# Value products of the expert layer: the order of the halves of gathered rows, and the count that frees their slots

## The chip, the cores and the metric

The kernel runs on one core of one Trainium2 chip, everything in 32-bit floats. The metric is the device time of one launch in microseconds, as the median of repeated runs. The engines are named as the profile names them: PE is the tensor engine's matmul, PEld its weight load, DVE the vector engine, ACT the scalar engine, POOL the GpSimd engine, SP the queue that issues the loads of weights.

## The reference, cut to what matters

The reference is a two-layer decoder trunk for 256 prompt tokens and 8 sample tokens of width 1024. In each layer a mixer (matrix-memory LSTM heads and causal pooling) is followed by an expert layer and by a gated per-layer embedding. The change touches the expert layer alone, which picks 16 single-neuron experts in each of 8 heads of every token out of tables of 16384 rows:

```python
def block_fn(xb):                                   # 128 tokens
    ...
    eidx = jnp.take_along_axis(cidx, sel, axis=-1)  # token, head, 16
    gate = jax.nn.softmax(top, axis=-1)
    ue = u_tab[eidx]
    act = jax.nn.gelu(jnp.einsum('td,thkd->thk', xb, ue).astype(jnp.float32))
    ve = v_tab[eidx]
    return jnp.einsum('thk,thkd->td', (gate * act).astype(xb.dtype), ve)
```

So every token needs 128 rows of `u` (a dot product each) and 128 rows of `v` (their weighted sum). The rows of 1024 floats come from HBM by index.

## The kernel before

**Tiles and passes.** The tokens of a layer are three tiles: A (tokens 0 to 127), B (128 to 255) and S (the 8 samples). Over the two layers they are tiles 0 to 5. The expert layer runs in four passes: tile 0; tiles 1 and 2; tile 3; tiles 4 and 5. In each pass all gathers of `u` come first, then all of `v`.

**Gathers.** POOL issues 1056 gathers in the fixed order `GATHERS` (the loop from line 1427, the DMA at 1450). One gather brings 128 rows of 1024 floats, one for each partition, 512 KB, into slot n % 14 of the ring `rows` (`RING` = 14). Below, "a row" is the content of one such slot. For `u`, row i holds expert i of each of the tile's 128 tokens. For `v`, the index is transposed: one row holds the 128 experts of one token. Gather n raises `row_in[n % 14]` by 16 when it has landed. Before POOL issues gather n it waits until the slot's last content, gather n - 14, has been used: by the count `u_used`, which DVE raises with each row (line 2105), or by the count `v_used`, which PE raises. `V_BY` (lines 617 to 620) counts for every gather how many `v` rows there are up to it; before the change POOL turns that into groups of four (line 1447).

**Dots.** DVE multiplies a `u` row by the normalised tokens and sums it (line 2105), one instruction for each row.

**Value products.** `vals(t, g)` (lines 1196 to 1237) handles `GROUP` = 4 rows, thus four tokens. PE waits until all four have landed (lines 1212 and 1213). Row i's product is a matmul with 32 columns of weights in `wz`, of which one is not zero, so that the sum lands in one partition of `acc`; the four rows of a group write to the four blocks of 32 partitions. `acc` has 1024 columns in two PSUM banks of 512, so each row takes two matmuls, its first half (c = 0) and its second half (c = 1). All four first halves come first, then all four second halves, and the last matmul raises `v_used` by one for the group:

```python
for c in range(2):
    for i in range(GROUP):
        ...
ins.then_inc(v_used, 1)
```

Each such fp32 matmul shows in the trace as two MATMUL and two weight-load records, 16 MATMULs to a group. There are 122 groups of this kind (32 for each of tiles 0, 1 and 3, and 26 for tile 4). The last 6 groups of tile 4 ("late") and the two groups of each S tile go another way (lines 1214 to 1229): each row is four matmuls of 256 columns, one for each block of 32 partitions, and again one raise of `v_used` for a group. These are 10 groups.

**Who waits for `v_used`.** POOL before it reuses a slot (line 1447); DVE's `refill` (line 2140) after group 16 of a tile, when it puts the second half of the weights into `wz`; DVE's `gelu` of an S tile and its `weights`, which wait for an earlier tile's last group; and `add_experts` (line 2144), which adds `acc` to the residual once `all_added(t)` (lines 632 and 633) is reached.

**What sets the order.** Every engine runs a list of steps (`SCHEDULE`) that a planner has woven from step costs when the kernel is built: "vals" is taken as 1.8 us of PE, "dots" as 1.31 us of DVE for each row, and a slot is taken as free at the end of its group (lines 477 to 480). While tile 0's and tile 3's `v` rows are summed, PE and DVE also work through the next tiles' mixer, queries and expert choice, with weights that SP loads into a ring of three 1 MB slots. In the last part of tile 1's and tile 4's `v` rows PE has nothing else to do.

Of the kernel before, what the change touches and what calls it, by code (L numbers as in the profile page):

```python
# [30 lines left out]
BLOCK = 512  # L31
# [11 lines left out]
RING = 14  # L43
GROUP = 4
DOTS = 2
QUAD = 32
TURN = QUAD // 2
# [65 lines left out]
def layer_of(tile):  # L113
    return tile // 3
# [147 lines left out]
def own_groups(t):  # L262
    late = LATE if t == PASS_TILES[-1][0] else 0
    return ROWS_V[KIND[t]] // GROUP - late
# [34 lines left out]
PLACE = {g: n for n, g in enumerate(GATHERS)}  # L299
# [281 lines left out]
def count(stages, entry):  # L581

    n = 0
    for e in SCHEDULE:
        n += e[0] in stages
        if e == entry:
            return n
    raise KeyError(entry)


def chosen_by(tile, head):

    n = 0
    for e in SCHEDULE:
        n += e[0] == ("choose" if KIND[tile_of(e)] == "S" else "best") if e[0] in ("best", "choose") else 0
        if e[:2] == ("choose" if KIND[tile] == "S" else "best", tile) and e[2] <= head < e[3]:
            return n
    raise KeyError(tile)
# [18 lines left out]
U_BY, V_BY = [], []  # L617
# [5 lines left out]
def token(tile, i):  # L623

    return i if KIND[tile] == "S" else QUAD * (i % 4) + i // 4
# [4 lines left out]


def all_added(tile):
    return V_BY[PLACE["v", tile, own_groups(tile) * GROUP - 1]] // GROUP


def lane_of(tile, i):

    if KIND[tile] == "S":
        return i
    return DEC + LATE * (i % GROUP) + i // GROUP - own_groups(tile)  # L640
# [28 lines left out]
def build(nc, a):  # L669
    with ExitStack() as ctx:  # L670
        def sb(name, *shape, dt=F32):
            return ctx.enter_context(nc.sbuf_tensor(name, list(shape), dt))

        def sem(name):
            return ctx.enter_context(nc.semaphore(name))
# [3 lines left out]
        rows = sb("rows", P, RING, D)  # L679
# [24 lines left out]
        v = {"A": sb("v", P, HEADS, HD + 1), "S": sb("v_s", P, HD + 1)}  # L704
# [69 lines left out]
        wz = sb("wz", P, 4, TURN * (QUAD + 1) + TURN)  # L774
# [3 lines left out]
        acc = ctx.enter_context(nc.psum_tensor("acc", [P, 2, BLOCK], F32))  # L778
# [14 lines left out]
        half_used, u_used, v_used = sem("half_used"), sem("u_used"), sem("v_used")  # L793
# [27 lines left out]
        def lane_group(g):  # L821
            return slice(g * LANE, (g + 1) * LANE)
# [9 lines left out]
        def window(g, lane):  # L832

            return (QUAD + 1) * (g % TURN) + TURN - lane
# [8 lines left out]
        def emptied(eng, *name):  # L843

            b, n = use[name]
            eng.wait_ge(bank_free[b], n + 1)  # L846

        @block.tensor
        def _(pe):
# [346 lines left out]
            def vals(t, g):  # L1196

                kind = KIND[t]
                if g == 0:
                    if kind != "S":  # L1200
                        emptied(pe, "turn_w", t)
                    else:
                        pe.wait_ge(weight_done, t + 1)
                    if t > 0:
                        pe.wait_ge(acc_read, t)
                if kind != "S" and g == TURN:
                    pe.wait_ge(refilled, count(("refill",), ("refill", t)))
                late = g >= own_groups(t)
                if late:
                    pe.wait_ge(acc_read, t + 1)  # L1210
                n = PLACE["v", t, g * GROUP]
                for i in range(GROUP):
                    pe.wait_ge(row_in[(n + i) % RING], 16 * ((n + i) // RING + 1))
                if kind == "S" or late:
                    lanes_from = own_groups(PASS_TILES[-1][0]) if layer_of(t) == DEPTH - 1 else 0
                    first = g == (lanes_from if late else 0) and (late or not lanes_from)
                    for i in range(GROUP):
                        row = rows[:, (n + i) % RING, :].rearrange("p (c s n) -> p c s n", c=2, s=4)
                        lane = lane_of(t, g * GROUP + i)
                        if late:  # L1220
                            at = window(g, lane)
                            weights_of = wz[:, i, at:at + LANE]
                        else:
                            weights_of = wz_s[:, lane * LANE:(lane + 1) * LANE]
                        for s in range(4):
                            ins = pe.matmul(acc[lane_group(s), 0, 0:HALF], weights_of, row[:, :, s, :],
                                            start=first and i == 0, stop=kind == "S" and lane == DEC - 1, skip_group_check=True)
                    ins.then_inc(v_used, 1)
                    return
                first, end = g == 0, g + 1 == own_groups(t)  # L1230
                for c in range(2):
                    for i in range(GROUP):
                        row = rows[:, (n + i) % RING, c * BLOCK:(c + 1) * BLOCK]
                        at = window(g, g)
                        ins = pe.matmul(acc[i * QUAD:(i + 1) * QUAD, c, :], wz[:, i, at:at + QUAD], row,  # L1235
                                        start=first, stop=end, skip_group_check=True)
                ins.then_inc(v_used, 1)

            def turn3(t):
                pe.wait_ge(acc_read, t + 1)  # L1240
# [185 lines left out]
        @block.gpsimd  # L1426
        def _(pool):
            pool.memset(wz[:, :, :], 0.0).then_inc(wz_clear, 1)
            pool.memset(wz_s[:, :], 0.0).then_inc(wz_clear, 1)
            for n, (table, t, i) in enumerate(GATHERS):  # L1430
                kind = KIND[t]
                if kind == "S" and table == "u" and i == 0:
                    emptied(pool, "turn_s", t)
                if kind != "S" and table == "u" and i % TOPK == 0:

                    pool.wait_ge(index_ready, chosen_by(t, i // TOPK))
                if kind != "S" and table == "v" and i == 0:
                    emptied(pool, "turn_index", t)
                if n >= RING:

                    old = GATHERS[n - RING]
                    if old[0] == "u" and KIND[old[1]] == "S":
                        emptied(pool, "copies", old[1], old[2], 1)
                    elif old[0] == "u":
                        pool.wait_ge(u_used, U_BY[n - RING])
                    else:
                        pool.wait_ge(v_used, (V_BY[n - RING] + GROUP - 1) // GROUP)
                at = i if table == "u" else token(t, i)
                which = index[kind] if table == "u" else index_t[kind]
                pool.indirect_dma_start(  # L1450
                    out=rows[:, n % RING, :], out_offset=None, in_=a[table],
                    in_offset=bass.IndirectOffsetOnAxis(ap=which[:, at:at + 1], axis=0),
                ).then_inc(row_in[n % RING], 16)
# [233 lines left out]
        def _(dve):  # L1687
# [422 lines left out]
            def gelu(t):  # L2110

                kind = KIND[t]
                dve.wait_ge(gelu_done, t + 1)
                if t == 0:
                    dve.wait_ge(wz_clear, 2)
                if kind == "S":
                    if t > 2:
                        dve.wait_ge(v_used, all_added(t - 3))
                    by_token = wz_s[:, :].rearrange("p (b c) -> p b c", c=LANE + 1)[:, :, 0:1].rearrange("p b o -> p (b o)")
                    after(dve.tensor_tensor(by_token, dots["S"][:, :], prob["S"][:, :], ALU.mult), weight_done)  # L2120
                    return
                after(dve.tensor_tensor(dots[kind][:, :], dots[kind][:, :], prob[kind][:, :], ALU.mult), weight_done)

            def by_token():
                placed = wz[:, :, TURN:].rearrange("p j (r c) -> p j r c", c=QUAD + 1)[:, :, :, 0:1]
                return placed.rearrange("p j r o -> p j (r o)")
# [10 lines left out]

            def refill(t):

                dve.wait_ge(v_used, V_BY[PLACE["v", t, TURN * GROUP - 1]] // GROUP)  # L2140
                after(dve.tensor_copy(by_token(), w_later[:, :, :]), refilled)  # L2141

            def add_experts(t):
# [181 lines left out]
```

## Time and profile before

| what | value |
|---|---|
| median of 3 runs | 1913.62 us (1909.67 to 1915.09) |
| span of the profiled execution | 1891.7 us |
| PE busy | 1079.0 us, 57% of the span |
| DVE busy | 978.1 us, 52% |
| POOL busy | 998.2 us, 53% |
| DMA queue of the gathers | 75.9% of the 16 DMA engines' span |
| HBM traffic | 362 GB/s over the span |
| mean granted TensorE clock | 0.752 of full |

The page gives the span of the profiled execution, from its first to its last instruction, and no time of its own beside it. The median lies 21.9 us above that span, which is what lies around the instructions, and the scatter from run to run. No engine is busy for 60% of the span, while the DMA engines' share is at 9 tenths or just under in most of the page's 40 slices. The stretches with `v` rows are, in us of the span: tile 0's rows from 340 to about 570; tile 1's from about 810 to 996; tile 3's from 1250 to 1472; tile 4's from 1696 to 1870, the last of them late groups and the S rows of tile 5.

### The profile page before, as it was taken

How to read it: one execution, taken by the hardware profiler on the slowest of the kernel's cores; microseconds unless marked ns; L12 is line 12 of the kernel's file. 1: busy time of each engine (PE TensorE's matmuls, PEld its weight loads, DVE VectorE, ACT ScalarE, POOL GpSimd, SP SyncE). 2: the span in 40 equal slices, each digit the busy share in tenths (PEclk: the TensorE clock that was granted, in tenths of full speed). 3: DMA queues.
4: the chain of work that ended last, by engine and by line, in shares of the span. 5: the costliest groups of instructions: out<-in, count | busy, mean ns of one | idle time of the engine just before them, and what ended most of it. 6: DMA issues, size and time to landing. Idle time of an engine off the chain costs nothing. (4 is left out here: it accounts for less than half of the span.)

```text
span 1891.7 us, 17959 instructions
## 1 busy us (share of the span) xinstructions
PE 1079.0 (57%) x6318; PEld 499.7 (26%) x6318; DVE 978.1 (52%) x2585; ACT 192.3 (10%) x332; POOL 998.2 (53%) x1062
## 2 busy tenths in 40 slices
PE   8840257788955835385655874048885522045556
PEld 4420133433412422241112432024341211031113
DVE  1498975523445788954004576951344497850001
ACT  3200021201101200000000212000110000000002
POOL 0156534345465555656666353755446566656663
PEclk9965668789987967697676886578896765576678
DMA  8699869889999999989999799979999999999995
GB/s 333 244 359 379 337 244 410 337 359 399 357 360 406 423 410 421 404 343 419 371 366 386 256 421 365 408 286 418 368 337 366 402 374 381 396 330 372 368 367 206
DMA packets 172759, 685.11 MB, mean 362 GB/s; under 512 B 19616, under 2 KB 21344, under 8 KB 158190
## 3 DMA queue, kind: packets, MB, share of 16 engines
q0 software_dynamic: 152064, 553.72, 75.9%
q1 hardware_dynamic: 20606, 130.25, 17.3%
q8 instruction: 51, 0.84, 0.2%
q14 instruction: 38, 0.31, 0.0%
HBM read 677.66 MB, written 6.59 MB: 362 GB/s over the span
## 5 line engine op out<-in xcount | busy, mean ns | idle before, releaser
L2105 DVE SCALAR_TENSOR_TENSOR rows<-rows,acc 128x1024 f32<-128x1024 f32 x512 | 594.2, 1217 | 49.6 <-issue 26.7
L908 PE MATMUL bank<-wring,turned 128*128 128x512 f32 (+1 forms) x808 | 394.0, 635 | 40.6 <-DMA wring<-in_w 24.3
L1235 PE MATMUL acc<-rows,wz 128*32 128x512 f32 x1952 | 323.1, 783 | 143.6 <-DMA rows<-in_v,index_tb 102.6
L1450 POOL DMA_INDIRECT rows<-in_u,index_A x256 | 240.3, 939 | 303.2 <-DVE rows L2105 123.8
L1450 POOL DMA_INDIRECT rows<-in_v,index_ta x256 | 242.5, 947 | 234.1 <-PE acc L1235 142.2
L1450 POOL DMA_INDIRECT rows<-in_u,index_B x256 | 240.7, 940 | 179.1 <-DVE rows L2105 110.7
L1450 POOL DMA_INDIRECT rows<-in_v,index_tb x256 | 241.1, 942 | 138.7 <-issue 68.1
L908 PEld LDWEIGHTS bank<-wring,turned 128*128 128x128 f32 x808 | 160.5, 207 | 236.7 <-issue 205.7
L1235 PEld LDWEIGHTS acc<-rows,wz 128*32 128x32 f32 x1952 | 69.6, 130 | 351.9 <-issue 347.0
L1185 PE MATMUL bank<-xn_s,consts 128*128 128x128 f32 x256 | 48.6, 334 | 154.3 <-issue 154.3
L1185 PEld LDWEIGHTS bank<-xn_s,consts 128*128 128x128 f32 x256 | 42.9, 243 | 159.9 <-issue 159.9
L2151 DVE TENSOR_TENSOR x_b<-x_b,acc 128x1024 f32<-128x1024 f32 x2 | 2.4, 1222 | 155.8 <-issue 89.9
L905 PE MATMUL bank<-wring,turned_s 128*32 128x128 f32 x1568 | 64.9, 281 | 27.1 <-issue 27.0
L1959 DVE MAX8 top<-scratch 128x8 f32<-128x128 f32 x66 | 15.0, 282 | 120.9 <-ACT scratch L1604 119.6
L905 PEld LDWEIGHTS bank<-wring,turned_s 128*32 128x32 f32 x1568 | 44.8, 111 | 69.7 <-issue 69.6
L2141 DVE COPY wz<-w_later 128x64 f32<-128x64 f32 x4 | 0.9, 225 | 101.4 <-PE acc L1235 77.7
L1109 PE MATMUL bank<-consts,qk 128*128 128x128 f32 x64 | 12.5, 324 | 68.7 <-issue 66.3
L1194 PE MATMUL bank<-consts,dots_A 128*128 128x128 f32 x2 | 1.0, 476 | 76.6 <-issue 74.6
L2105 DVE DVE_READ_ACCUMULATOR rows<-rows,acc 128x1 f32 x512 | 42.0, 82 | 3.6 <-issue 3.6
L1136 PE MATMUL bank<-consts,top 128*128 128x128 f32 (+2 forms) x10 | 3.9, 393 | 61.9 <-DVE top_f L1993 61.9
L1259 PE MATMUL bank<-wring,emb 128*128 128x512 f32 x32 | 19.9, 781 | 26.8 <-issue 13.6
L2169 DVE TENSOR_TENSOR xn<-xn,bank 128x512 f32<-128x512 f32 x6 | 4.1, 689 | 59.9 <-PE bank L1259 59.9
(320 smaller groups left out, 1054.4 us busy)
## 6 DMA issues: line engine op xcount, KB each, us to landing
wring<-in_w SPq DMA_DIRECT2D x103, 1024.0 KB
out_sample<-scratch SPq DMA_DIRECT2D x2, 2128.5 KB
scratch<-in_c_s SPq DMA_DIRECT2D x2, 2064.0 KB
rows<-in_u,index_A POOLq DMA_INDIRECT x256
rows<-in_v,index_ta POOLq DMA_INDIRECT x256
rows<-in_u,index_B POOLq DMA_INDIRECT x256
rows<-in_v,index_tb POOLq DMA_INDIRECT x256
kept<-in_w SPq DMA_DIRECT2D x2, 1024.0 KB
```

The source lines that it names most:

```text
L905: ins = pe.matmul(ps[lane_group(g), 0:P], turned["S"][:, 4 * h + c, :], w[:, c, g * P:(g + 1) * P], start=first, stop=end, skip_group_chec ...
L908: ins = pe.matmul(ps[:, part], turned["A"][:, 4 * h + c, :], w[:, c, part], start=first, stop=end, skip_group_check=True)
L1109: ins = pe.transpose(ps[:, i * P:(i + 1) * P], pq[:, 0, i * P:(i + 1) * P], const("ident"))
L1136: ins = pe.transpose(ps[0:m, i * P:(i + 1) * P], src[:, 2 * h0:2 * h1, :].rearrange("p l k -> p (l k)"), const("ident"))
L1185: ins = pe.matmul(ps[:, g * P:(g + 1) * P], const("ident")[:, lane:lane + 1].to_broadcast([P, P]), xn["S"][:, i * P:(i + 1) * P], start=Tr ...
L1235: ins = pe.matmul(acc[i * QUAD:(i + 1) * QUAD, c, :], wz[:, i, at:at + QUAD], row, start=first, stop=end, skip_group_check=True)
L1259: ins = pe.matmul(ps[:, :], emb[:, c, 0:P], w[:, 2 * j + c, :], start=(c == 0), stop=(c == 1))
L1450: pool.indirect_dma_start(out=rows[:, n % RING, :], out_offset=None, in_=a[table], in_offset=bass.IndirectOffsetOnAxis(ap=which[:, at:at + ...
L1959: highest = [marked(dve.max(values[:, 0:half], src)) for values, _, src in lists]
L2105: dve.scalar_tensor_tensor(u, u, 1.0, acc[:, :, :], ALU.mult, ALU.mult, accum_out=dots[kind][:, s:s + 1]).then_inc(u_used, 1)
L2151: after(dve.tensor_tensor(sum_, sum_, acc[:, :, :], ALU.add), acc_read)
L2169: free(dve.tensor_tensor(sig, sig, ps[:, 0:n], ALU.mult), "embed", t, j)
```

## The change

Three things change, and no other instruction, load or step is added, removed or moved:

1. `v_used` counts rows instead of groups. `all_added` and the waits of POOL and of `refill` are rewritten for that.
2. In the 122 ordinary groups PE waits for each row just ahead of its first half. The eight matmuls come in the order (row, half): (0,0) (1,0) (0,1) (2,0) (1,1) (3,0) (2,1) (3,1), and each second half raises `v_used`.
3. In the late groups and the groups of the S tiles PE waits for each row ahead of its four matmuls, and `v_used` is raised after each row.

```diff
 def all_added(tile):
-    return V_BY[PLACE["v", tile, own_groups(tile) * GROUP - 1]] // GROUP
+    return V_BY[PLACE["v", tile, own_groups(tile) * GROUP - 1]]
...
-                for i in range(GROUP):
+
+                def landed(i):
                     pe.wait_ge(row_in[(n + i) % RING], 16 * ((n + i) // RING + 1))
+
                 if kind == "S" or late:
...
                         lane = lane_of(t, g * GROUP + i)
+                        landed(i)
                         if late:
...
-                    ins.then_inc(v_used, 1)
+                        ins.then_inc(v_used, 1)
                     return
                 first, end = g == 0, g + 1 == own_groups(t)
-                for c in range(2):
-                    for i in range(GROUP):
-                        row = rows[:, (n + i) % RING, c * BLOCK:(c + 1) * BLOCK]
-                        at = window(g, g)
-                        ins = pe.matmul(acc[i * QUAD:(i + 1) * QUAD, c, :], wz[:, i, at:at + QUAD], row,
-                                        start=first, stop=end, skip_group_check=True)
-                ins.then_inc(v_used, 1)
+                at = window(g, g)
+
+                def half_product(i, c):
+                    row = rows[:, (n + i) % RING, c * BLOCK:(c + 1) * BLOCK]
+                    return pe.matmul(acc[i * QUAD:(i + 1) * QUAD, c, :], wz[:, i, at:at + QUAD], row,
+                                     start=first, stop=end, skip_group_check=True)
+
+                for i in range(GROUP):
+                    landed(i)
+                    half_product(i, 0)
+                    if i:
+                        half_product(i - 1, 1).then_inc(v_used, 1)
+                half_product(GROUP - 1, 1).then_inc(v_used, 1)
...
-                        pool.wait_ge(v_used, (V_BY[n - RING] + GROUP - 1) // GROUP)
+                        pool.wait_ge(v_used, V_BY[n - RING])
...
-                dve.wait_ge(v_used, V_BY[PLACE["v", t, TURN * GROUP - 1]] // GROUP)
+                dve.wait_ge(v_used, V_BY[PLACE["v", t, TURN * GROUP - 1]])
```

## Rows read from the trace of the kernel before

**Rows 1.** The page: busy time by engine, and the gathers' queue.

```profile
PE 1079.0 (57%) x6318; PEld 499.7 (26%) x6318; DVE 978.1 (52%) x2585; ACT 192.3 (10%) x332; POOL 998.2 (53%) x1062
...
q0 software_dynamic: 152064, 553.72, 75.9%
```

**Rows 2.** The page, costliest groups: line, engine, tiles, busy us, mean ns, idle before.

```profile
L1235 PE MATMUL acc<-rows,wz 128*32 128x512 f32 x1952 | 323.1, 783 | 143.6 <-DMA rows<-in_v,index_tb 102.6
```

**Rows 3.** The waits of the whole span: us in total, times, longest us.

```profile
POOL rows L1450 <- PE acc L1235: 171.0, 49, 13.3
```

**Rows 4.** Windows: length, PE, PEld, DVE, ACT, POOL busy (instructions), clock, DMA share, GB/s.

```profile
340.00:520.00 180.00, 149.00 (x1109) 71.48 (x1113) 69.27 (x282) 24.58 (x48) 83.27 (x88) 0.91 0.93 360
...
880.00:996.00 116.00, 63.52 (x344) 13.07 (x339) 1.45 (x2) 0.00 (x0) 76.41 (x82) 0.72 0.98 375
...
1600.00:1656.00 56.00, 0.66 (x2) 0.23 (x1) 46.40 (x79) 0.00 (x0) 36.60 (x40) 0.50 1.01 400
```

**Rows 5.** Windows of line 1235 alone: PE and PEld busy, clock, DMA share, GB/s.

```profile
340.00:520.00 180.00, 52.04 (x360) 11.70 (x364) 0.91 0.93 360
520.00:570.00 50.00, 24.50 (x156) 5.42 (x148) 0.79 0.97 358
...
880.00:996.00 116.00, 63.48 (x340) 12.99 (x332) 0.72 0.98 375
1250.00:1420.00 170.00, 51.83 (x368) 12.04 (x368) 0.89 0.92 352
1420.00:1472.00 52.00, 27.48 (x148) 5.48 (x144) 0.67 0.98 372
1696.00:1827.00 131.00, 70.57 (x368) 14.48 (x368) 0.70 0.97 369
```

**Rows 6.** The waits between 340 and 520 us.

```profile
POOL rows L1450 <- PE acc L1235: 73.8, 15, 13.3
```

**Rows 7.** The waits between 880 and 996 us.

```profile
PE acc L1235 <- DMA rows<-in_v,index_tb: 43.7, 17, 5.0
...
POOL rows L1450 <- remote: 13.4, 5, 3.3
...
POOL rows L1450 <- PE acc L1235: 4.4, 3, 2.6
```

**Rows 8.** The timeline of POOL in the stretch of tile 4.

```profile
1739.03 0.93 POOL L1450 DMA_INDIRECT rows<-in_v,index_tb  x1 [0.31 <-issue]
1743.36 0.94 POOL L1450 DMA_INDIRECT rows<-in_v,index_tb  x1 [3.39 <-PE acc L1235]
...
1766.20 0.93 POOL L1450 DMA_INDIRECT rows<-in_v,index_tb  x1 [3.29 <-PE acc L1235]
```

**Rows 9.** The timeline of POOL in the u stretch before it.

```profile
1645.92 0.94 POOL L1450 DMA_INDIRECT rows<-in_u,index_B  x1 [0.46 <-DVE rows L2105]
```

**Rows 10.** The timeline of PE: start, duration, count of instructions, idle before.

```profile
380.17 5.36 PE L1235 MATMUL acc<-rows,wz 128*32 128x512 f32 x48
...
1734.56 3.64 PE L1235 MATMUL acc<-rows,wz 128*32 128x512 f32 x16 [2.45 <-issue]
1739.47 3.64 PE L1235 MATMUL acc<-rows,wz 128*32 128x512 f32 x16 [1.26 <-issue]
```

**Rows 11.** The timeline of PE at the end.

```profile
1824.51 1.92 PE L1235 MATMUL acc<-rows,wz 128*32 128x512 f32 x16 [2.58 <-DMA rows<-in_v,index_tb]
...
1869.40 3.64 PE L1226 MATMUL acc<-rows,wz_s 128*32 128x256 f32 x32 [4.86 <-DMA rows<-in_v,index_S]
1876.75 3.39 PE L1226 MATMUL acc<-rows,wz_s 128*32 128x256 f32 x32 [3.71 <-DMA rows<-in_v,index_S]
```

**Rows 12.** The timeline of POOL at the end.

```profile
1849.71 1.40 POOL L1450 DMA_INDIRECT rows<-in_v,index_tb  x1 [4.26 <-PE acc L1226]
```

**Rows 13.** The timeline of DVE at the end.

```profile
1834.47 1.22 DVE L2151 TENSOR_TENSOR x_b<-x_b,acc 128x1024 f32<-128x1024 f32 x1 [65.89 <-remote]
...
1880.25 0.42 DVE L2146 TENSOR_TENSOR x_s<-x_s,acc 128x256 f32<-128x256 f32 x1 [14.89 <-PE acc L1226]
```

## The prediction

> **What bounds the kernel now.** I first read the page's busy times [rows 1]. No engine is near its span, while the queue of the gathers takes 75.9% of the DMA engines' time. Line 1235, the value products, has PE idle 143.6 us ahead of it, 102.6 of them until tile B's rows land [rows 2], while POOL waits 171.0 us in 49 pieces for those products to free slots [rows 3]. So each waits for the other, in different places. The average hides two kinds of stretch, so I read it by windows next [rows 4], then for line 1235 alone [rows 5].
>
> In the **woven** stretches, 340 to 520 and 1250 to 1420 us, PE is busy 149.00 of 180 us with the next tiles' work and the value products are a third of that (52.04). No wait of line 1235 on a DMA shows among the waits there; instead POOL waits 73.8 us for the products to free slots [rows 6]. The rows are there before PE is, and PE's own list of steps sets the pace. In the **landing-paced** stretches, 520 to 570, 880 to 996, 1420 to 1472 and 1696 to 1827, PE has only the products, is busy 63.52 of 116 us, and waits 17 times, 43.7 us in sum, for a row to land [rows 4, 7]. The DMA share is 0.97 to 0.98. By MATMUL records these stretches hold (156 + 340 + 148 + 368) / 4 = 253 rows [rows 5], four records to a row. All of tile 1's and tile 4's ends lie on the path that sets the end.
>
> The pace there is 82 gathers in 116 us, 1.415 us a row [rows 4]; between two marks of POOL 16 gathers apart, 1743.36 and 1766.20, it is 22.84 / 16 = 1.43 [rows 8]. POOL could issue every 0.93 + 0.31 = 1.24 us, and once in 16 gathers it stands still for 3.3 us, released by PE or by a source the trace calls remote [rows 7, 8]. The question is whether that stop costs anything. The gather stream without PE answers it in part: in the u stretch from 1600 to 1656 slots are freed row by row, and 40 gathers take 56 us, 1.40 us each, with a short wait at each one [rows 4, 9]. So freeing by the row changes the shape of the waiting, from one long stop to many short ones, and the rate hardly.
>
> **Part one, slots freed by the row, landing-paced stretches.** A group's passes now begin with the landing of its fourth row, and all slots come free 3.64 us later at the low clock [rows 10]. After the change the first row is used while the others still land. Its slot comes free about 4 us sooner, the second and third less, the fourth not at all. POOL has 14 slots in flight; a group that is waiting or being used holds at most four rows and 3.64 us of landing, under three more, so at least seven transfers are still queued. DMA engines that have seven transfers waiting don't stand still. The gain then is 1.42 less 1.40 for 253 rows: 0.02 x 253 = 5 us. The bounds are 0 (the pace is the engines' own) and 253 x (1.42 - 1.24) = 45 us (POOL's own pace). I take 5, since the u row is the nearest to it: the same size of gather, the same ring, and one signal for each row. By the late signals it would be more: the group whose slot POOL wants at 1743.36 had ended before 1739.47, so the stop is partly a signal that arrives late. Row-by-row signals may be just as late.
>
> **Part two, the order of the halves.** The work is the same: eight matmuls, 16 records. At the low clock a group takes 3.64 us for 16 records of 1.06 us each at most, so the four blocks of 32 partitions run side by side, in four rounds of 0.9 us; at the high clock three groups in a row take 5.36 us, 1.79 each, 0.45 a round [rows 10]. The skewed order still has four records for each block, so four rounds are the least. In the landing-paced stretches the first three rows' rounds move into time in which PE idles now. The fourth row needs its four rounds after it has landed as before, so a group's end doesn't move, unless the clock does. The granted clock is 0.72 there [rows 4], a mean over times at 1.2 and at 2.4 GHz, with PE stopping for 1.3 to 2.8 us between groups. With rows used as they land the stops are shorter and more; the clock could be granted for longer. The gain is at the ends of tiles: at most 3.64 - 1.92 = 1.7 us at each of four [rows 10, 11], nothing where the last group is fast already, as tile 4's is (1.92 at 1824.51). I take 1.5 us for all.
>
> In the woven stretches all four rows are there, so nothing starts sooner and all four blocks finish in the same round: I put the order and the earlier signals at nothing. POOL's 73.8 us of waiting there [rows 6] is for PE's other work, and rows that come in sooner only lie longer. That is covered by PE's list; if products ran one after another instead, the first slot would come free up to three quarters of 1.79 us sooner and POOL's waits would shrink, still without moving PE.
>
> **Part three, late and S groups.** POOL waits for whole groups of line 1226, 4.26 us at 1849.71 [rows 12], and what comes last is the landing of the S rows: PE waits 4.86 and 3.71 us for them [rows 11], and DVE's last addition follows at 1880.25 [rows 13]. Freed by the row, the first slot of a group opens about three quarters of its length sooner, 1.4 us by the 1.92 us of a fast group [rows 11]. PE also uses S rows 0 to 2 of a group while the fourth lands, but the end needs the fourth. I take 1.5 us, between 0 and 4.
>
> **Part four, the waits and the signals.** 396 raises of a count are added, three in each of 132 groups. PE's four waits are the same four. A wait now stands between matmuls; what is queued behind it in the group's list is the second half of a row that has landed, (1,1) behind the third row and so on, and in the woven stretches nothing waits. A raise is priced by no row. Its bounds: 0, and the 0.13 us by which a single fast group (1.92) exceeds one of a packed three (1.79) [rows 10, 11]. I take 0: in the landing-paced stretches it lies in idle time, and a raise by another block's matmul need not hold the rest.
>
> The Trainium skill speaks against this part: "TensorE: Matmul & The Clock Gate", section "The cost: per-tile semaphore tail", has each raise take 26.3 ns one after another and advises one on the last matmul. By that rule 396 raises would be 10.4 us, an estimate, and the sum would be 1916. No row of this trace has several raises in one group, so it neither confirms nor refutes it.
>
> **The sum.** -5 - 1.5 - 1.5 = -8 us. The profiled execution goes from 1891.7 to 1883.7; the median of runs lies 21.9 above its span, and 1913.6 - 8 = 1905.6, say 1906. From no change, a measurement of this kernel tells about 0.3%, 5.7 us.
>
> **The rivals.** *Stops that cost their length.* If the 3.3 us stops do bind, the gathers speed up to what the engines can carry. From 1600 to 1656 they moved 400 GB/s, against 375 [rows 4]; 0.524 MB at 400 GB/s is 1.31 us, 0.11 less than now, 28 us over 253 rows, and with the 3 us of the other parts the time is 1883. For it: the stop has the length of two and a half gathers, and the DMA engines have carried more than they do here. Against it: the share is 0.98 already, the extra in that stretch was loads of weights, and the gathers were at 1.40. 0.15.
>
> *Slower: the order costs PE rounds.* The four blocks run side by side only if PE reaches past matmuls that wait for their block. Now the fourth block's first record stands behind three that can't start yet; in the skewed order (3,0) stands behind seven (the second records of (0,0), (1,0), (2,0), both of (0,1) and of (1,1)). If PE doesn't reach so far, the fourth block starts two rounds late and a group takes six rounds. That is 2 x 0.45 = 0.9 us for each of (360 + 368) / 16 = 45 woven groups, 41 us, in stretches where PE is busy for 83% and its list sets the pace [rows 4, 5]; with half of it hidden in PE's pauses, +20, so 1926. In the landing-paced stretches it is hidden. It decides from about 0.3 us a group upwards, where it passes the gain. For it: the order of issue is all that makes the blocks overlap. Against it: PE does overlap four blocks across three packed groups. 0.18.
>
> The Trainium skill, page "TensorE: Matmul & The Clock Gate", section "The mechanism" of the part on packing small matmuls, has matmuls start and end strictly in the order of issue. In this order two records of one block follow each other, so a strict order would need nine rounds for a group, 4.0 us by 0.45, and the packed three took 1.79 each [rows 10]: the trace disagrees, and so this rule doesn't count against the new order either.
>
> *The raises cost.* Half of the upper bound, 0.065 x 3 in 45 woven groups, 9 us: 1915. 0.10, half of it beyond what counts as no change.
>
> *Nothing.* The engines carry what they can (share 0.98), the ends don't move, 1913. POOL's waits change shape only. 0.17.
>
> **How the numbers follow.** My forecast, 1906, has 0.40, a fifth of it within 5.7 us of no change. Faster: 0.32 + 0.15 = 0.47. Within: 0.08 + 0.17 + 0.05 = 0.30. Slower: 0.18 + 0.05 = 0.23. The range reaches to the first rival below, 1880, and to the second above, 1925; left out are more than that gain and the slow order at more than half its price. The likeliest case alone spans 1899 to 1911.
>
> **What would show it.** In the profile after: the stops at every 16th gather gone and POOL's waits short and many; gathers from 880 to 996 and from 1696 to 1827 at 1.40 us a row (my forecast), 1.31 or less (the first rival) or 1.42 (nothing); woven groups at 1.79 us in a row of three, or 2.7 (the slow order); the clock in the landing-paced stretches; DVE's addition of tile 4 at about 6 us before 1834.47. I am wrong if the woven stretches change in length by more than 3 us, or the GB/s of the landing-paced ones passes 385.

## The result and the profile after

The changed kernel takes 1933.82 us (median of 4 runs, 1929.70 to 1940.54) beside 1911.64 us for the kernel before in the same comparison. The ratio is 1.0092, with a 95% interval of 1.0047 to 1.0138: slower by about 1%, where I had forecast 1906 us and 0.4% faster. Two more comparisons on other occasions gave 1.0105 (1.0056 to 1.0155) and 1.0108 (1.0061 to 1.0155). One profiled execution scatters by about as much as the effect: the changed kernel's three profiles span 1938.7, 1903.1 and 1919.7 us. So single rows of one profile show here how something happens, and only ratios say what it costs. The profiled execution of 1938.7 us took 1940.54 us by its own time, 1.8 us more than its span; the 21.9 us that the forecast added to the span of the profile before were therefore mostly scatter between executions.

The page after, as in [rows 1, 2], with the value products now at line 1238:

```profile
PE 1155.1 (60%) x6318; PEld 519.0 (27%) x6318; DVE 978.1 (50%) x2585; ACT 192.3 (10%) x332; POOL 997.8 (51%) x1062
...
q0 software_dynamic: 152064, 553.72, 75.1%
...
L1238 PE MATMUL acc<-rows,wz 128*32 128x512 f32 x1952 | 394.3, 671 | 61.8 <-issue 31.8
```

PE is busy 76 us longer, nearly all of it in the products (323.1 to 394.3 us). Their idle time fell more than that, from 143.6 to 61.8 us, and nothing was won. Over the whole span POOL waits a little longer for the products than in [rows 3], in 77 pieces instead of 49:

```profile
POOL rows L1459 <- PE acc L1238: 194.5, 77, 11.5
```

The windows of the same stages: tile 0's woven stretch, and the landing-paced ones of tiles 1 and 4 (columns as in [rows 4]):

```profile
355.00:535.00 180.00, 143.94 (x1052) 66.36 (x1053) 61.71 (x240) 19.45 (x38) 77.60 (x82) 0.87 0.88 327
907.00:1023.00 116.00, 92.49 (x332) 17.59 (x324) 0.23 (x1) 0.00 (x0) 76.56 (x82) 0.97 0.98 374
1742.00:1873.00 131.00, 102.93 (x365) 20.36 (x362) 0.22 (x1) 0.00 (x0) 85.87 (x92) 0.96 0.97 366
```

In the landing-paced stretch of tile 1 there are again 82 gathers in 116 us, at 374 GB/s (375 before) and a share of 0.98: the same number of gathers in the same time as in [rows 4]. PE is busy 92.49 us there instead of 63.52 and its clock is granted at 0.97 instead of 0.72. For line 1238 alone (to be held against [rows 5]):

```profile
355.00:535.00 180.00, 52.01 (x336) 12.76 (x336) 0.87 0.88 327
907.00:1023.00 116.00, 92.49 (x332) 17.59 (x324) 0.97 0.98 374
```

The timelines show how. In the landing-paced stretch PE now starts with each row, so it hardly stops and stays at the high clock:

```profile
939.49 1.05 PE L1238 MATMUL acc<-rows,wz 128*32 128x512 f32 x4 [0.18 <-DMA rows<-in_v,index_tb]
940.71 1.05 PE L1238 MATMUL acc<-rows,wz 128*32 128x512 f32 x4 [0.17 <-DMA rows<-in_v,index_tb]
941.97 2.28 PE L1238 MATMUL acc<-rows,wz 128*32 128x512 f32 x8 [0.20 <-issue]
```

POOL's one stop of 3.3 us in 16 gathers [rows 8] has become several of 1.4 to 2.1 us, the rate is unchanged:

```profile
946.74 0.94 POOL L1459 DMA_INDIRECT rows<-in_v,index_tb  x1 [1.54 <-PE acc L1238]
949.56 0.94 POOL L1459 DMA_INDIRECT rows<-in_v,index_tb  x1 [1.88 <-remote]
...
958.14 0.93 POOL L1459 DMA_INDIRECT rows<-in_v,index_tb  x1 [1.40 <-remote]
...
967.42 0.94 POOL L1459 DMA_INDIRECT rows<-in_v,index_tb  x1 [2.13 <-remote]
```

In the woven stretch three groups in a row take 5.38 us, against 5.36 in [rows 10]. The skewed order costs PE nothing; but 18 us later PE waits 8.55 us for ACT:

```profile
390.90 5.38 PE L1238 MATMUL acc<-rows,wz 128*32 128x512 f32 x48
...
408.50 1.92 PE L1089 MATMUL bank<-pooled_s,w_pool 128*128 128x32 f32 x8 [8.55 <-issue]
```

That wait is where I first saw something of the loss. Here are the two pieces of ACT's work that release these matmuls (the pooling of tile B and of the samples), in the kernel before:

```profile
358.57 0.60 ACT L1569 ACTIVATE decayed<-bank 128x512 f32<-128x512 f32 x1 [5.72 <-PE bank L1078]
...
390.94 0.28 ACT L1569 ACTIVATE pooled_s<-bank 128x128 f32<-128x128 f32 x1 [3.77 <-PE bank L1067]
```

and after:

```profile
370.69 0.60 ACT L1578 ACTIVATE decayed<-bank 128x512 f32<-128x512 f32 x1 [11.18 <-remote]
...
408.17 0.28 ACT L1578 ACTIVATE pooled_s<-bank 128x128 f32<-128x128 f32 x1 [10.27 <-remote]
```

PE's last matmul of the first group of inputs (line 1078) and the matmul that waits for ACT:

```profile
364.14 0.29 PE L1078 MATMUL bank<-consts,u_a 128*128 128x16 f32 x2
371.35 2.08 PE L1089 MATMUL bank<-decayed,w_pool 128*128 128x128 f32 x8 [6.91 <-ACT decayed L1578]
```

PE's input for ACT's step was done at 364.14 + 0.29 = 364.43 us, and ACT began at 370.69, 6.3 us later. The profile finds no instruction that ended just before, and calls the releaser "remote". PE then stood 6.91 us. The trace's semaphore events settle what ACT waited for: the count that PE's matmul raises changed at 370.61 us. The completion of a matmul was reported six microseconds after its end. The second time the matmul ended at 399.95 and its raise was seen at 408.09, 8.1 us late. POOL was in an unbroken run of 12 gathers, which ends at 407.68, and ACT started at 408.17:

```profile
393.07 0.94 POOL L1459 DMA_INDIRECT rows<-in_v,index_ta  x1 [10.16 <-PE acc L1238]
394.31 0.93 POOL L1459 DMA_INDIRECT rows<-in_v,index_ta  x1 [0.30 <-issue]
...
406.74 0.94 POOL L1459 DMA_INDIRECT rows<-in_v,index_ta  x1 [0.30 <-issue]
```

The same at the end of tile 0: the last product ends at 587.40 + 1.90 = 589.30, DVE's addition starts at 597.79.

```profile
587.40 1.90 PE L1238 MATMUL acc<-rows,wz 128*32 128x512 f32 x6 [1.05 <-DMA rows<-in_v,index_ta]
599.07 1.33 PE L884 MATMUL bank<-consts,x_a 128*128 128x128 f32 x5 [9.76 <-DVE x_a L2160]
```

```profile
597.79 1.22 DVE L2160 TENSOR_TENSOR x_a<-x_a,acc 128x1024 f32<-128x1024 f32 x1 [20.78 <-remote]
```

```profile
594.00 0.94 POOL L1459 DMA_INDIRECT rows<-in_u,index_B  x1 [0.30 <-issue]
597.79 0.93 POOL L1459 DMA_INDIRECT rows<-in_u,index_B  x1 [2.86 <-remote]
```

The semaphore events show the raises of `v_used` too. Here are those at that place, with the ends of the matmuls that make them and POOL's gathers (worked out from the trace, in us):

```
matmul ends    584.57 584.57 584.60 584.61   586.28 586.35 588.45 589.30
raise seen     586.21 587.66 589.80 591.91   597.53 597.59 597.65 597.70
gathers begin  585.31 586.55 587.80 589.04 590.28 591.52 592.76 594.00, stop, 597.79
```

While POOL issues, the raises come out singly, 1.4 to 2.1 us apart, up to 7.3 us late. After POOL has stopped, four come within 0.17 us, the oldest of them 11.3 us late. Over tiles 0 and 1 of the kernel before, a raise whose matmul ended during a run of gathers was seen 2.4 us late on average, one outside a run 0.4; after the change it was 4.2 and 0.9. (Raises and ends were paired in order; about 7% of the raises are missing from the trace, so these are estimates.) This rise lies in tile 1: by another pairing, the one with the least sum of delays, an estimate too, raises in a run were 2.8 us late in tile 1 before the change and 5.1 after, but 1.9 and 2.7 in tile 0. The experiments find no loss in tile 1 (e6 below), so the rise from 2.4 to 4.2 is not a measure of the loss.

### The profile page after: what moved, and what is told of

It is laid out like the page before. It is cut to its first block and busy times, and to the rows that moved or that the text cites. A ratio compares the mean times of both kernels' runs of the same rounds, so it can differ in the third digit from the quotient of the medians.

```text
span 1938.7 us, 17710 instructions
## 1 busy us (share of the span) xinstructions
PE 1155.1 (60%) x6318; PEld 519.0 (27%) x6318; DVE 978.1 (50%) x2585; ACT 192.3 (10%) x332; POOL 997.8 (51%) x1062
## 5 line engine op out<-in xcount | busy, mean ns | idle before, releaser
L1238 PE MATMUL acc<-rows,wz 128*32 128x512 f32 x1952 | 394.3, 671 | 61.8 <-issue 31.8
L1238 PEld LDWEIGHTS acc<-rows,wz 128*32 128x32 f32 x1952 | 87.0, 117 | 325.5 <-issue 204.1
L905 PE MATMUL bank<-wring,turned_s 128*32 128x128 f32 x1568 | 76.6, 290 | 45.8 <-issue 45.7
L905 PEld LDWEIGHTS bank<-wring,turned_s 128*32 128x32 f32 x1568 | 48.8, 115 | 93.0 <-issue 92.7
L1136 PE MATMUL bank<-consts,top 128*128 128x128 f32 (+2 forms) x10 | 3.9, 393 | 63.5 <-DVE top_f L2002 62.1
L1658 ACT ACTIVATE turned<-bank 128x512 f32<-128x512 f32 x8 | 4.8, 597 | 303.8 <-issue 161.3
L1120 PE MATMUL bank<-keys,q_t 128*128 128x128 f32 x128 | 22.5, 327 | 14.1 <-issue 10.8
```

The lines of the kernel that those rows point to most:

```text
L905: ins = pe.matmul(ps[lane_group(g), 0:P], turned["S"][:, 4 * h + c, :], w[:, c, g * P:(g + 1) * P], start=first, stop=end, skip_group_chec ...
L1120: ins = pe.matmul(ps[:, i * P:(i + 1) * P], pqT[:, i, :], keys[:, 4 * block_of(j) + i, :], start=True, stop=True)
L1136: ins = pe.transpose(ps[0:m, i * P:(i + 1) * P], src[:, 2 * h0:2 * h1, :].rearrange("p l k -> p (l k)"), const("ident"))
L1238: return pe.matmul(acc[i * QUAD:(i + 1) * QUAD, c, :], wz[:, i, at:at + QUAD], row, start=first, stop=end, skip_group_check=True)
L1658: free(act.activation(turned[KIND[t]][:, i * c:(i + 1) * c, :], ps[:, 0:c * m].rearrange("p (h c) -> p h c", h=c), ACT.Copy), "turn3", t, i)
```

## The experiments

All ratios are to the kernel before, from runs of the same comparison, with 95% intervals. "By the row" means one raise of `v_used` for each row, "by the group" one for four.

**The parts of the change alone.** e1 takes the changed kernel's raises and slots with the old order:

```diff
                 for i in range(GROUP):
                     landed(i)
-                    half_product(i, 0)
-                    if i:
-                        half_product(i - 1, 1).then_inc(v_used, 1)
-                half_product(GROUP - 1, 1).then_inc(v_used, 1)
+                for i in range(GROUP):
+                    half_product(i, 0)
+                for i in range(GROUP):
+                    half_product(i, 1).then_inc(v_used, 1)
```

> The old order and the old wait for four rows, but each second half raises the count and slots are freed by the row (396 more raises, slots as in the changed kernel). Theory 1, the raises: PE's completions already reach POOL and DVE several us late at the ends of tiles, and more raises make them later, for everybody who waits on PE; the ratio to before is that of the change, 1.008 to 1.014, about 1930 us. Theory 2, the order with its waits between matmuls: no loss, 0.997 to 1.002. Theory 3, slots freed earlier send gathers into the loads of weights: as theory 1 here, 1.008 to 1.014.

Measured: 1.0116 (1.0067 to 1.0164). The whole loss, without the new order.

e2 is the mirror: the new order and its waits, one raise for each group, `V_BY[...] // GROUP` in the waits as before.

```diff
-                        half_product(i - 1, 1).then_inc(v_used, 1)
+                        half_product(i - 1, 1)
```

> The new order with its waits row by row, but one raise for each group as before. Theory 1 (raises): no loss, 0.995 to 1.001. Theory 2 (order and waits): the whole loss, 1.008 to 1.014. Theory 3 (slots freed earlier): no loss.

Measured: 0.9994 (0.9961 to 1.0028). The order costs nothing and brings nothing. Theory 2 is out.

e3 is e1, but POOL waits for all four raises of a group:

```diff
-                        pool.wait_ge(v_used, V_BY[n - RING])
+                        pool.wait_ge(v_used, (V_BY[n - RING] + GROUP - 1) // GROUP * GROUP)
```

> The old order and waits, four raises for each group, but POOL waits for all four, so slots come free as before and only the number of raises differs. Theory 1 (raises): the whole loss, 1.008 to 1.014. Theory 2 (order): none, 0.998 to 1.002. Theory 3 (slots freed earlier): none.

Measured: 1.0033 (0.9991 to 1.0074). Theory 1 as I had put it falls too: the same raises as in e1 cost between nothing and 0.7% when POOL still waits for whole groups, not the whole loss; the value lies between the ranges of the theories. Freeing slots by the row makes up the rest, 0.8% by the middle values.

e4 is the changed kernel once more:

> The changed kernel once more, beside before on one chip. All theories: 1.005 to 1.014, and a second profile of it. Theory 1 expects again that DVE's additions at the ends of tiles 0 and 3 start 6 us or more after the last product, where before they followed within 0.2 us; if they don't, these late signals are chance.

Measured: 1.0105 (1.0056 to 1.0155). In its profile DVE's addition comes 4.9 us after the last product of tile 0 and 8.8 after that of tile 3: late again, though less than the 6 us that I had expected for tile 0.

**Where it costs.** e5 and e6 count by the row in some tiles only, with the new order everywhere. In e5:

```diff
+def BY_ROW(t, i):
+    return t in (0, 3)
...
-    V_BY.append((V_BY or [0])[-1] + (_g[0] == "v"))
+    V_BY.append((V_BY or [0])[-1] + (_g[0] == "v" and (BY_ROW(_g[1], _g[2]) or _g[2] % GROUP == 0)))
```

and the raises in `vals` to match; in e6 `t not in (0, 3)`.

> The changed kernel, but a raise and a free slot for each row only in tiles 0 and 3, whose products are woven with other work; tiles 1, 4 and the S tiles raise once a group. The new order stays everywhere. Theory A (PE's completions leave in order and slowly while POOL issues gathers, so extra raises delay the completions that ACT, DVE and POOL wait for; this costs where other engines wait on PE, in the woven stretches): nearly the whole loss, 1.007 to 1.013. Theory B (each extra raise costs the same wherever it stands): half of it, 1.004 to 1.006. Theory C (the loss comes from the landing-paced stretches and tile 4's end): 0.998 to 1.002.

> The mirror image: by the row in tiles 1, 4 and the S tiles, once a group in tiles 0 and 3. Theory A: 0.996 to 1.003. Theory B: 1.004 to 1.006. Theory C: 1.007 to 1.013. If it is below 0.997, freeing by the row pays where only the gathers set the pace.

Measured: e5 1.0108 (1.0060 to 1.0156), e6 1.0009 (0.9982 to 1.0036). The whole loss is in tiles 0 and 3, where other engines wait for PE while POOL gathers. In tiles 1 and 4, where the gathers set the pace, freeing by the row costs and gains nothing that can be told, at most 0.2%; most of my forecast's 5 us lay there.

e7 raises the count with all eight matmuls of a group, in the old order, POOL waiting for whole groups:

```diff
-                    half_product(i, 0)
+                    half_product(i, 0).then_inc(v_used, 1)
```

> The old order and waits, all eight matmuls of a group raise the count, and POOL waits for the whole group: 122 x 4 = 488 raises more than with four for a group (which gave 1.0033). Theory A and B, the raises themselves: 1.006 to 1.015. Theory D (what costs is that slots come free early, by the row, and the raises nothing): 1.000 to 1.004, as with four raises.

Measured: 1.0051 (1.0019 to 1.0082). It lies between the ranges of the theories, so it decides neither way.

e8 is the kernel before, again:

> The kernel before once more: 0.998 to 1.002 by every theory. Its second profile tells whether completions of PE at the ends of tiles 0 and 3 come late in it too (in the first profile DVE's additions followed the last product within 0.2 us; with the new order and one raise, 6 us or more late).

Measured: 0.9957 (0.9924 to 0.9989), which misses what an unchanged kernel should give: a difference of 0.4% can be chance in these comparisons. So e3 and e7 suggest that the raises themselves cost something, but don't show it. Its profile also takes away a reading of mine: late completions are in the kernel before as well. PE's two waits for ACT at the place of the first trace, in e8:

```profile
370.48 2.08 PE L1089 MATMUL bank<-decayed,w_pool 128*128 128x128 f32 x8 [6.30 <-ACT decayed L1569]
...
402.25 1.92 PE L1089 MATMUL bank<-pooled_s,w_pool 128*128 128x32 f32 x8 [2.54 <-ACT pooled_s L1569]
```

6.30 and 2.54 us, against 6.91 and 8.55 after the change; in the first profile of before they were 1.73 and 1.84. The two waits sum to 7.6 to 15.5 us with slots by the row in tile 0 (after, e1, e4, e5, e16) and to 3.6 to 11.4 by the group (before, e2, e3, e6, e7, e8); these overlap, and the later e13, by the row and with the whole loss, has only 4.4. So these two waits show the mechanism and do not measure the loss. DVE's addition at the end of tile 0 was about 8 us late in e8 and e2 too, so late ends of tiles don't set the two kernels apart.

A wider sum sets them further apart, though not cleanly. Over tiles 0 and 3, I add up from the trace the time by which instructions of ACT and DVE started after the last matmul that they waited for, where nothing else released them. This estimate is 86 to 108 us in six profiles by the row (after, e1, e4, e5, e13, e16; mean 98) and 67 to 100 in six by the group (before, e2, e3, e6, e7, e8; mean 87).

**Does POOL's run of gathers do it?** After e8 the theory was this: a completion of PE that falls into an unbroken run of gathers is held up. By the group, POOL stands until all four rows' work is reported, and in the stop all that is waiting gets out. By the row, POOL starts again with the first raise, and what is behind it, the other raises and the completions for ACT and DVE, comes out between gathers. The theory can be tried by making POOL pause, which at first sight can only cost time. e9 and e10 put 14 small memsets, each waiting for the one before, into an unused tile, after every 8th gather of rows 0 to 79 of tiles 0 and 3; e9 in the kernel before, e10 in the changed one:

```diff
                 ).then_inc(row_in[n % RING], 16)
+                if table == "v" and t in (0, 3) and i < 80 and i % 8 == 7:
+                    for _ in range(14):
+                        paused += 1
+                        pool.memset(spare[:, :], 0.0).then_inc(pauses, 1)
+                        pool.wait_ge(pauses, paused)
```

> The kernel before; POOL pauses (14 small memsets one after another, an estimate of 3 us) after every 8th gather of v rows 0 to 79 of tiles 0 and 3, ten pauses each. Theory A (completions of PE that fall into an unbroken run of gathers are held up, in the traces 2.4 us on average against 0.4 outside a run, most until up to 3 us after its end): shorter runs let them out, the first halves of tiles 0 and 3 get no longer, 0.992 to 1.001. Rival (the lateness has nothing to do with POOL's runs; slots are refilled later): 1.001 to 1.010.

> The changed kernel with the same pauses. Theory A: a good part of the loss of 1.0105 comes back, 0.998 to 1.006. Rival (slots free by the row cost in another way than by long runs of gathers): 1.008 to 1.015.

Measured: e9 1.0006 (0.9979 to 1.0032), e10 0.9996 (0.9970 to 1.0021). The interval of e9 reaches into the ranges of both theories and decides nothing. But twenty pauses of 3.8 us in the changed kernel don't cost time, they give the whole 1% back (by 1.0105 and 1.0108 for the changed kernel in other comparisons). One of them, in POOL's timeline of e10:

```profile
352.52 1.27 POOL L1461 DMA_INDIRECT rows<-in_v,index_ta  x1 [0.30 <-issue]
353.78 3.26 POOL L1468 MEMSET to_boundary<- 128x96 f32 x14
357.58 0.94 POOL L1461 DMA_INDIRECT rows<-in_v,index_ta  x1 [0.55 <-POOL to_boundary L1468]
```

and PE's two waits for ACT in e10, now 0.75 and 1.43 us:

```profile
357.36 1.16 PE L1090 MATMUL bank<-decayed,w_pool 128*128 128x128 f32 x8 [0.75 <-ACT decayed L1585]
...
391.21 1.92 PE L1090 MATMUL bank<-pooled_s,w_pool 128*128 128x32 f32 x8 [1.43 <-ACT pooled_s L1585]
```

e11 leaves a gap after each of these gathers in the kernel before (`i < 80` alone as the condition, two memsets instead of 14), and e12 is the changed kernel with slots and raises by the group in the first 16 groups of tiles 0 and 3 (`BY_ROW` is `t not in (0, 3) or i >= 16 * GROUP`):

> The kernel before; two small memsets one after another (an estimate of 0.4 us) after every one of these gathers, so that no run is unbroken. Theory A: as the pauses or better if a gap after each gather lets completions out one by one, 0.992 to 1.001; the rival: 1.001 to 1.010.

> The changed kernel, with raises and slots by the group only in the first 16 groups of tiles 0 and 3, by the row everywhere else. By the traces so far these halves took 120.5 and 109.4 us with groups and 127.4 and 113.0 with rows, 10.5 of some 20 us lost. Theory A (loss where ACT waits on PE, in the mixer steps woven there): 0.999 to 1.005. Rival (the loss lies in the second halves and the ends of these tiles): 1.007 to 1.012.

Measured: e11 0.9978 (0.9951 to 1.0005), e12 1.0031 (0.9999 to 1.0063). By the middle value of e12 some two thirds of the loss are in the first halves, where the mixer of the next tiles is woven in.

**Broken runs or later refills?** A pause also lets slots be refilled later, as by the group. e13 pauses as often and as long, but mostly before gathers at which POOL stops anyway (in tile 0 after rows 13, 21, 25, 37, 41, 49, 57, 65, 69 and 77, in tile 3 after 13, 21, 29, 37, 41, 45, 53, 57, 69 and 77), so that the runs of gathers stay whole:

```diff
+                if table == "v" and t in (0, 3) and i < 80 and i in ((13, 21, ...) if t == 0 else (13, 21, ...)):
```

e14 puts e11's gap after each gather into the changed kernel.

> The changed kernel with ten pauses of 3.8 us in tile 0 and ten in tile 3 as in e10, but each just before a gather at which POOL has stopped in the traces anyway (rows 14, 22, 26, 38 and so on), so that no run of gathers is broken. Theory A (long runs hold up completions): the loss stays, 1.006 to 1.013. Rival (later refills give it back): 0.998 to 1.003.

> The changed kernel with two small memsets (0.7 us) after each gather of v rows 0 to 79 of tiles 0 and 3, so that every run is broken everywhere. Theory A: 0.996 to 1.002. If only stops of some us let completions out and short gaps don't: 1.006 to 1.012.

Measured: e13 1.0111 (1.0058 to 1.0165), e14 0.9999 (0.9968 to 1.0031). The pauses of e13 change nothing. But they do not test the later refills as I had meant: in the profile 13 of the 20 lie inside a stop that PE ended anyway, so they put off no refill, and the other seven put one off by some 3 us at most. e13 shows that the pauses in themselves give nothing back where they neither break a run nor put off a refill; e10 and e14 do both, and no run does one alone. POOL's timeline of e13 shows one that lies in a stop; after it POOL resumes at the first raise, as ever:

```profile
370.47 0.94 POOL L1461 DMA_INDIRECT rows<-in_v,index_ta  x1 [0.30 <-issue]
371.41 3.26 POOL L1468 MEMSET to_boundary<- 128x96 f32 x14
381.83 0.95 POOL L1461 DMA_INDIRECT rows<-in_v,index_ta  x1 [7.15 <-PE acc L1239]
383.08 0.94 POOL L1461 DMA_INDIRECT rows<-in_v,index_ta  x1 [0.30 <-PE acc L1239]
```

The gaps of e14 give everything back, against e16 in the same comparison. A gap of 0.97 us from the end of one gather to the start of the next is enough:

```profile
352.88 0.95 POOL L1461 DMA_INDIRECT rows<-in_v,index_ta  x1 [0.55 <-POOL to_boundary L1468]
353.82 0.43 POOL L1468 MEMSET to_boundary<- 128x96 f32 x2
354.80 0.95 POOL L1461 DMA_INDIRECT rows<-in_v,index_ta  x1 [0.55 <-POOL to_boundary L1468]
```

The sum of late starts of ACT and DVE over tiles 0 and 3, the estimate given above, falls to 50 us in e14 and to 46 and 35 in e11 and e15; with the pauses of e9 and e10 it is 69 and 77. PE's two waits for ACT in e14 are down to 0.75 and 0.43 us:

```profile
355.43 1.16 PE L1090 MATMUL bank<-decayed,w_pool 128*128 128x128 f32 x8 [0.75 <-ACT decayed L1585]
...
382.85 1.91 PE L1090 MATMUL bank<-pooled_s,w_pool 128*128 128x32 f32 x8 [0.43 <-ACT pooled_s L1585]
```

Two other ways by which earlier refills could cost time can be held against the traces. One is that gathers crowd out the loads of weights, which e1's expectation had as a third theory. In tiles 0 and 3 no profile has a wait of PE for such a load, and by the recorded landings each was in at least 3.4 us before its first use. The other is slower work of DVE or ACT beside the gathers: over tile 0 their instructions sum to between 122.7 and 123.4 us and to 31.2 or 31.3 us in all profiles.

e15 repeats e11, e16 the changed kernel:

> The same file as e11 (0.9978): between 0.995 and 1.001; below 0.998 with an interval under 1 would make it faster than both kernels.

> The changed kernel again: 1.008 to 1.013 by every theory, the measure for e13 and e14.

Measured: e15 0.9979 (0.9950 to 1.0009), e16 1.0108 (1.0061 to 1.0155). Held against e16 in the same comparison, e13 is the same and e14 1% better. The kernel before with gaps came out 0.2% faster twice; each interval reaches just over 1, and an unchanged kernel gave 0.9957 in e8, so it is not shown to beat the kernel before.

## Why the prediction was wrong

**Slots freed by the row, landing-paced stretches (-5 us forecast): nothing.** The mechanism was right and the size was not. I had reasoned that at least seven transfers are always queued, so the engines don't stand still, and then still granted 0.02 us a row from a u stretch. 82 gathers in 116 us before and after, and e6 at 1.0009 (0.9982 to 1.0036), say that the answer lies at the lower bound or close to it. The first rival (the stops cost their length, 1883 us) falls with it: the stops shrank to 1.4 to 2.1 us and the rate stayed.

**The order of the halves (0 forecast): right.** Packed groups take 5.38 us for three, e2 is at 0.9994. The rival on the slower side, rounds lost because PE can't reach past seven matmuls, did not happen; the sign I had given for being wrong, woven stretches longer by more than 3 us, came true for another reason. The nine rounds of a strict order didn't appear after the change either.

**The ends of tiles (-1.5 us).** The clock rose as I thought it could, 0.72 to 0.97, but what sets the end there is the landing and then the report of the last product, 8.5 us late at the end of tile 0 in this profile. No gain shows.

**The late and S groups (-1.5 us forecast): no gain shows.** From POOL's issue of the last row of tile 4's ordinary groups to the end of the span it is 73.6 and 69.7 us in the two profiles of the kernel before, and 75.7, 71.4 and 73.7 in the three of the changed one. The last rows still have to land: PE waits for the landing of each of the last three S rows (1.20, 0.67 and 0.40 us after the change).

**The woven stretches (0 forecast): this is the step that failed.** I wrote "I put the order and the earlier signals at nothing. POOL's 73.8 us of waiting there [rows 6] is for PE's other work, and rows that come in sooner only lie longer. That is covered by PE's list." It was not covered. From the first `v` gather of tile 0 to the 128th after it took 243.5 us before and 259.5 after, in tile 3 231.8 and 236.2; as means of the same six profiles by the group and six by the row, 249.4 and 254.1 us in tile 0, 232.5 and 239.8 in tile 3. That is 12 us of some 20. The waiting was not useless: in POOL's stops for a whole group PE's held-up completions get out. With slots by the row POOL goes on at the first raise, ACT and DVE hear from PE later (98 us in sum against 87, the means of the estimate above), PE waits for them, and the list that I had called the cover became longer. From e1 (1.0116) and e3 (1.0033), 0.8% hangs on when POOL resumes; from e5 and e6, all of the loss is in tiles 0 and 3; from e10 and e14, it goes when POOL's stream in their first 80 rows is broken up.

**The raises (0 forecast; rival 1915 us).** e3's 1.0033 and e7's 1.0051 point to a few us, but e8's 0.9957 for an unchanged kernel is as far from 1. The Trainium skill has 26.3 ns for a raise in "TensorE: Matmul & The Clock Gate", section "The cost: per-tile semaphore tail"; by it 396 raises would be 10.4 us, an estimate, 0.55%. e3 neither confirms nor refutes that sum. e7 does not bear it out: its 884 raises more than the kernel before would be 23 us, 1.2%, by the same figure, and it measured 0.5%, at most 0.8%. The three packed groups grew by 0.02 us with nine more raises, which is 2 ns each, so between packed groups PE's timeline shows no such tail.

I had seen the late signal, and named it for POOL's stop before 1743.36 ("the stop is partly a signal that arrives late"). I did not ask who else waits for PE's signals, nor what lets them out.

**What stays open.** Why a gap lets a completion of PE out isn't shown by any run: the trace has the events, not the path between the engines. Whether e10 and e14 give the loss back because runs are broken or because slots are refilled later is not separated by a run; the late starts that shrink with the gaps, and weights that land in time either way, speak for the first. How much of the loss is the count of raises and how much POOL's early resumption is known only as e3 leaves it, 0 to 0.7% for the raises.

## What to carry to other kernels

Finer signals were not free here, where completions are late while another engine issues an unbroken stream of gathers: before removing a coarse wait, ask what it does for everybody else. Where PE feeds ACT and DVE while POOL issues gathers back to back, compare the end of a matmul with the start of the instruction it releases; if they lie microseconds apart and the releaser is "remote", try a short gap between gathers where POOL has time to spare. And in this kernel a stretch at a DMA share of 0.98 gained nothing from slots that come free sooner (e6).

## What the runs showed of the hardware that I had not expected

- Completions of PE are late while POOL issues gathers at its full pace of 1.24 us: raises of `v_used` by 2.4 us on average in the kernel before and 4.2 after the change (the rise is tile 1's), 0.4 to 0.9 outside such runs. They come out singly between gathers, or all at once when POOL stops (four in 0.17 us).
- A pause in POOL's stream can make a kernel faster: 0.97 us between gathers in place of 0.30, for 160 gathers, took the changed kernel from 1.0108 to 0.9999.
- With rows used as they land, the same products in the same time ran at a granted clock of 0.97 instead of 0.72, and PE counts as busy 92.5 us instead of 63.5: a busier and faster PE in a stretch that got no shorter. It is the order that does it: over 116 us near the end of tile 1's gathers the clock is 0.69 in e1 (old order, raises by the row) and 0.96 in e2 (new order, one raise a group).
